# A hybrid decoder step on Trainium2: split operands of TensorE stored at other pitches

## The reference

```
p = rmsnorm(x) @ w_in                     # 2048 -> 7184
attention over 8 heads (blocks of 256 keys, paged cache for the 8 sequences)
gated delta rule over 8 heads (conv width 4, SiLU, chunks of 64 or 8, gated norm)
x = x + concat(attention, delta) @ w_out  # 2048 -> 2048
u = rmsnorm(x) @ w_up                     # 2048 -> 2 x 5632
x = x + (silu(conv(gate)) * conv(value)) @ w_down   # 5632 -> 2048
y = rmsnorm(x)
```

## Time and profile before

| | |
|---|---|
| median of the runs | 1656.75 us (1656.0, 1656.75, 1656.87) |
| profiled execution | span 1652.1 us, from its first to its last instruction; the page gives no other time of it |
| PE | 1631.9 us busy (99%), 12899 matmuls |
| DVE | 1047.0 us busy (63%) |
| ACT | 617.4 us busy (37%) |
| POOL | 237.2 us busy (14%) |
| granted clock of PE, mean | 0.997 of full speed |
| read from and written to device memory | 243.50 MB and 12.69 MB, 155 GB/s over the span |

### The profile page before, as it was taken

The page is one execution under the profiler, slowest core; times in us unless marked ns, Lnnn a source line. Parts: engine busy times, 40 slices in busy tenths (PEclk is TensorE's granted clock), DMA queues, the critical chain, the costliest instruction groups (busy, mean ns, idle before and its releaser), DMA issues.

```text
span 1652.1 us, 30918 instructions
## 1 busy us (share of the span) xinstructions
PE 1631.9 (99%) x12899; PEld 1583.0 (96%) x12899; DVE 1047.0 (63%) x1707; ACT 617.4 (37%) x786; POOL 237.2 (14%) x370
## 2 busy tenths in 40 slices
PE   8999999999999999999999999999999999999998
PEld 7999989988999998999999999999999999999997
DVE  5675688656544454776666666666666666666665
ACT  6444324432343343643333333333333333333334
POOL 1122342123212022210000000101010101010004
PEclk9999999999999999999999999999999999999998
DMA  8453355335857467454445444445444444445442
GB/s 251 128 154 111 103 151 159 106 116 147 255 184 257 131 204 233 128 157 149 154 141 158 148 154 152 146 149 153 150 147 151 152 149 147 153 141 157 149 154 84
DMA packets 231243, 256.64 MB, mean 155 GB/s; under 512 B 9444, under 2 KB 220966, under 8 KB 231104
## 3 DMA queue, kind: packets, MB, share of 16 engines
q1 hardware_dynamic: 217856, 220.10, 43.3%
q0 software_dynamic: 10560, 33.29, 6.4%
q10 hardware_dynamic: 2688, 1.27, 0.3%
HBM read 243.50 MB, written 12.69 MB: 155 GB/s over the span
## 4 chain that ended last, share of the span: by engine, by line
PE 97%; DVE 1%; DMA 1%; issue 0%; ACT 0%; SPq 0%; POOL 0%; DVEq 0%; POOLq 0%; ACTq 0%
PE ps_proj L1758 23%; PE ps_proj L1759 22%; PE ps_proj L1760 22%; PE ps_small L1758 6%; PE ps_small L1759 6%; PE ps_small L1760 6%; PE ps_small L1800 2%; PE ps_small L2038 1%; PE ps_small L1939 0%; PE ps_small L2029 0%; PE ps_proj L1800 0%; PE ps_small L1929 0%; PE ps_small L2117 0%; PE ps_small L2135 0%; DMA x_raw<-in_x_sample_dram 0%; PE ps_small L2004 0%
## 5 line engine op out<-in xcount | busy, mean ns | idle before, releaser
L1758 PE MATMUL ps_proj<-x_hi,w_hi 128*128 128x320 f32 x2432 | 766.5, 315 | 0.4 <-issue 0.4
L1760 PE MATMUL ps_proj<-x_hi,w_lo 128*128 128x320 f32 x2432 | 751.5, 309 | 0.0
L1759 PE MATMUL ps_proj<-x_lo,w_hi 128*128 128x320 f32 x2432 | 751.5, 309 | 0.0
L811 ACT ACTIVATE w_hi<-w_raw 128x1024 fp32r<-128x1024 f32 x408 | 432.1, 1059 | 739.8 <-PE ps_proj L1760 546.3
L1162 DVE TENSOR_TENSOR w_lo<-w_raw,w_hi 128x1024 fp32r<-128x1024 f32 x408 | 498.2, 1223 | 300.9 <-ACT w_hi L811 300.6
L1758 PEld LDWEIGHTS ps_proj<-x_hi,w_hi 128*128 128x128 f32 x2432 | 456.9, 188 | 14.8 <-issue 11.7
L1759 PEld LDWEIGHTS ps_proj<-x_lo,w_hi 128*128 128x128 f32 x2432 | 457.1, 188 | 1.0 <-issue 1.0
L1760 PEld LDWEIGHTS ps_proj<-x_hi,w_lo 128*128 128x128 f32 x2432 | 456.7, 188 | 0.0
L1758 PE MATMUL ps_small<-hid_hi,w_hi 128*128 128x320 f32 x704 | 218.0, 310 | 0.0
L1760 PE MATMUL ps_small<-hid_hi,w_lo 128*128 128x320 f32 x704 | 217.6, 309 | 0.0
L1759 PE MATMUL ps_small<-hid_lo,w_hi 128*128 128x320 f32 x704 | 217.5, 309 | 0.0
(11 more groups left out here) (346 smaller groups left out, 1211.8 us busy)
## 6 DMA issues: line engine op xcount, KB each, us to landing
w_raw<-in_w_up_dram SPq DMA_DIRECT2D x176, 512.0 KB, 3.6
w_raw<-in_w_in_dram SPq DMA_DIRECT2D x112, 512.0 KB, 4.0
w_raw<-in_w_down_dram SPq DMA_DIRECT2D x88, 512.0 KB, 3.6
w_raw<-in_w_out_dram SPq DMA_DIRECT2D x32, 512.0 KB, 4.0
k_pages<-in_cache_k_dram POOLq DMA_DIRECT2D x32, 256.0 KB, 3.6
v_pages<-in_cache_v_dram POOLq DMA_DIRECT2D x32, 256.0 KB, 4.2
state_s<-in_state_gdn_dram POOLq DMA_DIRECT2D x10, 512.0 KB, 5.5
out_ss_dram<-state_s POOLq DMA_DIRECT2D x8, 512.0 KB, 4.4
```

The costliest lines, as they stand in the source:

```text
L811: act.activation(whi[:, slot], raw[:, slot], ACT.Copy).then_inc(hi_done, 1)
L1758: pe.matmul(o, hi, rhs_hi[:, k0 + kk_, :], start=first and kk_ == 0, stop=False)
L1759: pe.matmul(o, hi, rhs_lo[:, k0 + kk_, :], start=False, stop=False)
L1760: ins = pe.matmul(o, lo, rhs_hi[:, k0 + kk_, :], start=False, stop=last and kk_ == CQ - 1)
```

## The change

Four groups of tensors get a larger pitch; what is stored in them and the instructions that use them stay.

- x_hi and x_lo: a tile of 320 elements every 324 (1296 bytes in place of 1280).
- hid_hi and hid_lo: a tile every 332 elements (1328 bytes).
- w_hi: a ring slot of 1024 elements every 1028 (4112 bytes in place of 4096).
- w_lo: a ring slot every 1032 elements (4128 bytes).

w_raw, gated_hi and gated_lo keep their pitch. Tensors placed behind a padded one move up: w_lo starts 64 bytes later, x_res and x_hi 192, x_lo 448, the constants and all that follows 704, hid_lo 1088. Within a slot and within a tile all elements stay contiguous. ACT and DVE operations that wrote several whole tiles of x or hid as one run now write one run for each tile; those that write a slot still write one run of 1024.

```diff
--- before.py
+++ after.py
@@ -468,12 +468,12 @@
 
     sp_ = Span(base)
     raw = sp_.put("w_raw", [P, RING, CQ, CC])
-    whi = sp_.put("w_hi", [P, RING, CQ, CC], F32R)
-    wlo = sp_.put("w_lo", [P, RING, CQ, CC], F32R)
+    whi_ = sp_.put("w_hi", [P, RING, CQ * CC + 4], F32R)
+    wlo_ = sp_.put("w_lo", [P, RING, CQ * CC + 8], F32R)
     xres = sp_.put("x_res", [P, KT, TOK])
     yo_at = sp_.at
-    xhi = sp_.put("x_hi", [P, KT, TOK], F32R)
-    xlo = sp_.put("x_lo", [P, KT, TOK], F32R)
+    xhi = sp_.put("x_hi", [P, KT, TOK + 4], F32R)[:, :, 0:TOK]
+    xlo = sp_.put("x_lo", [P, KT, TOK + 4], F32R)[:, :, 0:TOK]
     cst = sp_.put("consts", [P, CONSTS.shape[1]])
     small = sp_.put("small", [P, 640])
     pT = sp_.put("params_t", [P, 160])
@@ -564,8 +564,8 @@
     zhi = nc.alloc_sbuf_tensor_at("gated_hi", [P, 8, TOK], F32R, offset=mixer_at + 4 * 4 * TOK)
     zlo = nc.alloc_sbuf_tensor_at("gated_lo", [P, 8, TOK], F32R, offset=zz_at)
     fm = Span(work_at)
-    hhi = fm.put("hid_hi", [P, 2, 4, TOK], F32R)
-    hlo = fm.put("hid_lo", [P, 2, 4, TOK], F32R)
+    hhi = fm.put("hid_hi", [P, 2, 4, TOK + 12], F32R)[:, :, :, 0:TOK]
+    hlo = fm.put("hid_lo", [P, 2, 4, TOK + 12], F32R)[:, :, :, 0:TOK]
     facc = fm.put("ffn_acc", [P, 2, 2, 338])
     xn = fm.put("x_normed", [P, 2, 4, TOK])
     yo = nc.alloc_sbuf_tensor_at("y_rows", [P, 3, DM], F32, offset=yo_at)
@@ -577,6 +577,12 @@
     psA = nc.alloc_psum_tensor("ps_proj", [P, 4, 512], F32)
     psB = nc.alloc_psum_tensor("ps_small", [P, 4, 512], F32)
     b0, b1, b2, b3 = (psB[:, i, :] for i in range(4))
+
+    def high_part(slot):
+        return whi_[:, slot, 0:CQ * CC].rearrange("p (k n) -> p k n", k=CQ)
+
+    def low_part(slot):
+        return wlo_[:, slot, 0:CQ * CC].rearrange("p (k n) -> p k n", k=CQ)
 
     def C(name, n=P, m_=None):
         at, width = CONST_COLS[name]
@@ -808,7 +814,7 @@
                 act.wait_ge(raw_in[slot], use * 16 + 16)
                 if not isinstance(c, int) or c >= RING:
                     act.wait_ge(mm_done, c - RING + 1)
-                act.activation(whi[:, slot], raw[:, slot], ACT.Copy).then_inc(hi_done, 1)
+                act.activation(high_part(slot), raw[:, slot], ACT.Copy).then_inc(hi_done, 1)
 
             def silu_z(n):
                 name, p = PAIRS[n]
@@ -1159,7 +1165,7 @@
             def lo_part(c, slot):
 
                 dve.wait_ge(hi_done, c + 1)
-                dve.tensor_tensor(wlo[:, slot], raw[:, slot], whi[:, slot].bitcast(F32), ALU.subtract).then_inc(lo_done, 1)
+                dve.tensor_tensor(low_part(slot), raw[:, slot], high_part(slot).bitcast(F32), ALU.subtract).then_inc(lo_done, 1)
 
             def evac(n):
                 name, p = PAIRS[n]
@@ -1753,8 +1759,8 @@
                 for j in range(2):
                     o = out_bank[:, j, 0:TOK]
                     for kk_ in range(CQ):
-                        hi = whi[:, slot, kk_, j * P:(j + 1) * P]
-                        lo = wlo[:, slot, kk_, j * P:(j + 1) * P]
+                        hi = high_part(slot)[:, kk_, j * P:(j + 1) * P]
+                        lo = low_part(slot)[:, kk_, j * P:(j + 1) * P]
                         pe.matmul(o, hi, rhs_hi[:, k0 + kk_, :], start=first and kk_ == 0, stop=False)
                         pe.matmul(o, hi, rhs_lo[:, k0 + kk_, :], start=False, stop=False)
                         ins = pe.matmul(o, lo, rhs_hi[:, k0 + kk_, :], start=False, stop=last and kk_ == CQ - 1)
```

## The result

The change makes the kernel slower by a little: median 1660.56 us of seven runs (1659.57 to 1661.7) against 1656.87 us of seven before, ratio 1.0023 with a 95% interval of 1.0013 to 1.0032. The profiled execution's span is 1660.0 us; it is the slowest of the seven.

A forecast was written before the change was run, and what follows sets the result against it. The prediction took PE, through the 146.7 ns between product matmul starts, to bound the kernel. Its three terms summed 0 + 0 + 0 to a forecast median of 1656.75 us, with an eight-in-ten range of 1618 to 1669.

The forecast's parts named there:

- term 1: PE's moving and weight reads, 9408 matmuls with a moved moving operand: cost taken as 0, bounds -125 and +861 us.
- its own sign of being wrong: Distance between PE's matmul starts: the prediction is wrong if it moves by more than 0.35 ns in the mean.
- What bounds the kernel: PE, busy 99% of the span: 9792 product matmuls at 0.1467 us make 1436 of 1652.1 us.
- Terms 2 and 3: ACT's high and DVE's low part of each chunk, and writes to padded x and hid tiles: each taken as 0.
- The sum: Whole kernel: 0 + 0 + 0 on the median 1656.75 us, 4.65 us above the profiled span of 1652.1 us.
- A: PE's weight load and moving read collide; spreading starts breaks the 13.3 ns surplus: 31 us gained, 1625 us; chance 0.31.
- B: PE's moving reads starting inside a larger unit cost one more: +5.9 us, 1662.7 us, or +4.0, 1660.7; chance 0.23.
- C: Starts already differ enough or the padding is absorbed: same time; chance 0.46 together with the forecast.
- the likeliest case: The forecast of no change in the whole kernel, median 1656.75 us, with its own range 1654 to 1660.
- same: Whole kernel: no change that a measurement can tell, about 0.2% or 3.3 us; chance 0.46.

## Why the prediction was wrong

The step that failed is term 1: the cost of the moved operand reads was taken as 0. The mean distance between starts moved from 146.6 to 147.2 ns (800 us over 5457 and over 5435 matmuls), more than the 0.35 ns that the prediction named as its own sign of being wrong.

**What bounds the kernel** held: PE, by the distance between starts, without slack. A mean distance longer by 0.4% in the feed-forward part (3534 ns a chunk) showed in the time at once.

**Term 1.** It took 0 for 9408 matmuls with new moving addresses, on the ground that the pace was equal for x, hid and w_ab operands, as a fixed cost of swapping weights would be. It measured +19.3 ns for an x chunk and +3.1 ns for a hid chunk: in the feed-forward part 176 x 19.3 + 88 x 3.1 = 3.7 us (941.0 us against 937.4 in the traces), as much as the median difference of 3.7 us (2.2 to 5.3 by its interval). The feed-forward part is counted here from the first of its 264 chunks, at 701.8 us in the trace of before, and not at about 712. The mixer's 144 chunks were 4.1 us longer in this pair of profiles, but that stretch varies by 7 us between profiles of the full kernels. Between two split products in a row the mean distance there is 146.47 ns before and 146.72 after, some 3100 times, so about 0.8 us of it can be put down to the pace. The evidence was one layout seen many times: before, every operand stood at the same residue modulo 256 bytes (w_ab at that or 128 off), and the layout of before has one rhythm behind every start that was tried. Its evenness was the entrained state of that layout and not a constant of the matmul. How the two operands' addresses act inside PE is not shown: the runs show only that nothing else has to run for it. The trace had a hint that was read as flat: the w_ab starts, at two decimals in the earlier trace rows, are in ns 147, 151, 146, 149, 145, 145, 148, 145, 140 and 148 apart. The split products' own distances are 146 or 147 ns from the eighth behind a break on, with one exception, and w_ab is the only operand of this form at another residue.

**Terms 2 and 3 held.** w_hi 1060 ns, w_lo 1224, and the writers of the padded x tiles 1258 and 1493 ns against 1256 and 1492: four runs in place of one cost 1 to 2 ns.

**The sum.** Its 4.65 us are not what lies around the span. In every execution of a full kernel for which both are on record the time is 1.6 to 1.8 us above the span, so the profiled execution of before (span 1652.1 us) was itself about 3 us faster than the median. The forecast goes by the median and does not suffer, but the two profiled spans are 7.9 us apart where the medians are 3.7.

**The rivals.** A was nearest in mechanism: the pace hangs on the addresses of both operands, and the gaps depend on slot and tile as it said. That the two reads collide is its picture and was not seen, and it had the wrong sign for this layout. Its objection, that a different start need not keep the reads apart, did not hold in general: w_lo later by 128 bytes is enough for 144.4 ns. A gain of 31 us was named, and the best layouts gained 17 and 18. B had the sign and nearly the time (1662.7, or 1660.7 with its smaller unit), by luck: its pattern, three tiles of four slower, is not in the profile, and a start off a boundary can be faster (145.5 ns at 16 bytes). C is out, since the distances changed. The range (1618 to 1669) held the time because it reached into both rivals; the likeliest case's own range (1654 to 1660) just missed it. The prediction's own remark, that no row had a start between multiples of 64 bytes, was a reason for less than 0.46 on "same".

**The rules beside term 1.** The Trainium skill, "TensorE: Matmul & The Clock Gate", section on what happens when a matmul is issued, says that loading the next weights takes no read bandwidth from the running matmul. For these float32r operands that does not make the pace independent of where the weights lie: moving only the weights by 48 bytes can change it from 146.7 to 144.4 ns, on TensorE alone. Whether read bandwidth is what is lost, no run shows. The Trainium skill, "SBUF — State Buffer", section on the two sides, says PE waits on no other engine; here the runs agree, since the distances of the full kernel come back without the other engines.

## What to carry to other kernels

A kernel that TensorE bounds with equal, back-to-back matmuls should be tried at a few relative base addresses of its operands before its pace is called a constant (ACT and DVE showed no such effect in the ring operations here); a probe with that engine alone, in the kernel's order of reads, tells many layouts in one run. Prefer a constant shift that gives one good pace behind every start to pitches that walk through all residues: of the latter none went under 145.6 ns over its last two chunks, and the change's own reached 148.0. An even pace in a trace is evidence for the addresses in that trace and no others.

## What the runs showed of the hardware

- The distance between split-format matmuls of 320 columns depends on the residues modulo 256 bytes of the moving and the stationary operand: constant pairs ran from 144.4 to 153.3 ns on TensorE alone, at a granted clock of 1.00. The difference of the two residues alone does not give the figure.
- At some residues there are two stable rhythms at equal addresses, 433.3 and 440 ns for three matmuls (a few layouts had three figures), and what ran just ahead picks one until the next break. With both weights 48 bytes later, runs came at 1641 and at 1656 us, all with a mean granted clock of 0.997 or 0.998.
- Distances of 4 bytes count: both weights by 12 bytes gave 144.44 ns behind every start, by 4 bytes 147.9.
